# First stage of a hybrid attention block: scaling and copying x on ScalarE, small rows on ScalarE's DMA queue, gate weights loaded later and their products made up in steps 5 to 9

## What is computed

```
c_act = silu(c)
mod = c_act @ w_ada + b_ada
shift_m, scale_m, gate_m, shift_f, scale_f, gate_f = split(mod, 6)
h = rmsnorm(x, g_pre_mix) * (1.0 + scale_m) + shift_m
proj = h @ w_in
fq, fk, fv, ff, gq, gk, gv, ga, gr = split(proj, IN_OFFSETS)
log_f = log_sigmoid(ff + b_fgate)
cum = cumsum(log_f over the frames)      # bias of the attention logits: cum[q] - cum[k]
```

## Time and profile before

| | |
|---|---|
| three executions | 2312.43, 2312.89, 2318.76 us; median 2312.89 |
| profiled execution | 2309.94 us, of which the span (first to last instruction) is 2307.9 us |
| TensorE busy | 2173.3 us, 94% of the span |
| VectorE busy | 1520.3 us, 66% |
| ScalarE busy | 850.8 us, 37% |
| DMA | 441.09 MB, mean 191 GB/s |

### The profile page before, as it was taken

The page is one execution under the profiler, slowest core; times in us unless marked ns, Lnnn a source line. Parts: engine busy times, 40 slices in busy tenths (PEclk is TensorE's granted clock), DMA queues, the critical chain, the costliest instruction groups (busy, mean ns, idle before and its releaser), DMA issues.

```text
span 2307.9 us, 26312 instructions
## 1 busy us (share of the span) xinstructions
PE 2173.3 (94%) x9751; PEld 1769.3 (77%) x9751; DVE 1520.3 (66%) x1470; ACT 850.8 (37%) x1063; POOL 385.1 (17%) x217
## 2 busy tenths in 40 slices
PE   2778999999999999799999999999999999999996
PEld 2556877777777678688888888888878888888875
DVE  5855665666667732564454454454498989898998
ACT  2223323333333322443444343343344444444443
POOL 0000000000000000100000000000034545454664
PEclk9889999999999999899999999999999999999998
DMA  9855565555545342556666566566247664666763
GB/s 314 296 186 168 170 191 178 162 175 178 164 128 173 110 164 95 165 173 196 199 223 207 193 222 215 183 220 226 92 152 247 216 208 161 239 219 218 256 221 144
DMA packets 261821, 441.09 MB, mean 191 GB/s; under 512 B 17676, under 2 KB 110032, under 8 KB 255704
## 3 DMA queue, kind: packets, MB, share of 16 engines
q1 hardware_dynamic: 261128, 435.51, 56.6%
q10 hardware_dynamic: 592, 4.21, 0.5%
HBM read 379.88 MB, written 59.79 MB: 191 GB/s over the span
## 4 chain that ended last, share of the span: by engine, by line
PE 78%; issue 8%; DVE 7%; DVEq 2%; DMA 1%; SPq 1%; POOL 1%; ACT 1%; POOLq 0%; ACTq 0%
PE pair L737 25%; PE pair L739 24%; PE pair L738 24%; DVE am_acc L1721 3%; DVE v_op L1940 1%; DMA af_item<-in_w_ada 1%; PE pair L832 1%; DVEq L1720 1%; PE pair L811 1%; DVE w_lo L1485 0%; DVEq L1591 0%; PE pair L926 0%; POOL v_raw L2162 0%; PE pair L1008 0%; PE pair L872 0%
## 5 line engine op out<-in xcount | busy, mean ns | idle before, releaser
L737 PE MATMUL pair<-in_hi,w_hi 128*128 128x512 f32 x1792 | 725.3, 405 | 4.5 <-DVE grp L1496 2.5
L739 PE MATMUL pair<-in_hi,w_lo 128*128 128x512 f32 x1792 | 702.8, 392 | 0.0
L738 PE MATMUL pair<-in_lo,w_hi 128*128 128x512 f32 x1792 | 702.4, 392 | 0.0
L1485 DVE TENSOR_TENSOR w_lo<-w_raw,w_hi 128x2048 fp32r<-128x2048 f32 (+1 forms) x142 | 292.1, 2057 | 397.4 <-ACT w_hi L1101 396.8
L1101 ACT ACTIVATE w_hi<-w_raw 128x2048 fp32r<-128x2048 f32 (+1 forms) x142 | 244.7, 1723 | 461.6 <-PE pair L739 424.8
L737 PEld LDWEIGHTS pair<-in_hi,w_hi 128*128 128x128 f32 x1792 | 339.6, 190 | 86.3 <-issue 12.0
L739 PEld LDWEIGHTS pair<-in_hi,w_lo 128*128 128x128 f32 x1792 | 338.6, 189 | 73.3
L738 PEld LDWEIGHTS pair<-in_lo,w_hi 128*128 128x128 f32 x1792 | 339.6, 190 | 70.2 <-issue 2.6
L737 PE MATMUL pair<-v_op,hid_r 128*128 128x512 f32 x896 | 349.8, 390 | 5.8 <-DVE hid_r L1916 4.5
L738 PE MATMUL pair<-v_op,hid_r 128*128 128x512 f32 x896 | 349.2, 390 | 0.0
L739 PE MATMUL pair<-v_op,hid_r 128*128 128x512 f32 x896 | 349.1, 390 | 0.0
(11 more groups left out here) (205 smaller groups left out, 1880.3 us busy)
## 6 DMA issues: line engine op xcount, KB each, us to landing
w_raw<-in_w_mlp_in SPq DMA_DIRECT2D x64, 1024.0 KB, 5.3
v_raw<-in_w_mlp_out SPq DMA_DIRECT2D x128, 512.0 KB, 5.1
hid_r<-hid_scratch SPq DMA_DIRECT2D x112, 512.0 KB, 6.3
hid_scratch<-hid_r SPq DMA_DIRECT2D x28, 1792.0 KB, 7.2
am_item<-in_w_ada SPq DMA_DIRECT2D x64, 512.0 KB, 5.1
w_raw<-in_w_in SPq DMA_DIRECT2D x128, 256.0 KB, 3.4
af_item<-in_w_ada SPq DMA_DIRECT2D x64, 512.0 KB, 5.8
w_raw<-in_w_in SPq DMA_DIRECT2D x128, 128.0 KB, 3.2
```

Of the source, the lines that this page charges most:

```text
L737: pe.matmul(dst, a[0], b[0], start=start, stop=False, skip_group_check=onto)
L738: pe.matmul(dst, a[0], b[1], start=False, stop=False, skip_group_check=onto)
L739: return pe.matmul(dst, a[1], b[0], start=False, stop=stop, skip_group_check=onto)
L1485: dve.tensor_tensor(w_lo[n][:, view], w_raw[n][:, view], w_hi[n][:, view].bitcast(F32), ALU.subtract)\
```

## The change

1. The nine small row DMAs leave SP's queue and are issued by ScalarE as its first instructions. Their transposes use bank 5, and the x transposes wait for `cols_ready`.
2. ScalarE scales the four x tiles and copies all 16 transposed tiles out; VectorE does neither. VectorE has the block's eight items one after the other.
3. SP's order becomes: c, items and x as before up to item 7, then group 0's first weights (`load_fox(0, 0)`, 0.79 MB), item 8, the second weights, items 9 to 11, the two gate weight DMAs, and the rest.
4. The gate products of steps 0 to 4 are left out there and made up in steps 5 to 9, two in each. `wm_hi` moves to ahead of `modulate(4)`, `wm_lo` to the second block.
5. Item 16, block 2's first, is added ahead of `mod_columns_m(1)`, and item 24, block 3's first, ahead of `mod_columns_m(2)`. In blocks 1 to 3 the low part of the next weights stands right behind `mod_columns_m`, ahead of the first `in_lo`.
6. At the seam, `w_hi` and `w_lo` of group 1's first weights are made ahead of the `log_f` work, VectorE copies two tiles while it waits for the logarithm, and TensorE begins group 1's step 0 without `cum_ready`: it transposes `f_z` after three of the six tiles. Group 1 is written out instead of being the first pass of a loop.

```
@@ SP
-            load_am(2)
-            load_am(3)
-            for n, src in enumerate((g_pre_mix[0:1, :], b_ada[0:1, SHIFT_M:SHIFT_M + D],
...
-            load_am(4)
-            sp.wait_ge(wm_zero, 1)
-            sp.dma_start(wm_raw[:, :, 0:RANK], w_in_t[:, :, GA_COL:GA_COL + RANK]).then_inc(wm_in, 16)
...
+            for n in range(2, 8):
+                load_am(n)
             load_fox(0, 0, wait=False)
-            load_am(6)
-            load_am(7)
+            load_am(8)
             load_fox(0, 1, wait=False)
-            for n in range(8, 32):
+            for n in range(9, 32):
                 load_am(n)
+                if n == 11:
+                    sp.wait_ge(wm_zero, 1)
+                    sp.dma_start(wm_raw[:, :, 0:RANK], w_in_t[:, :, GA_COL:GA_COL + RANK]).then_inc(wm_in, 16)
@@ PE
             for k in range(KT):
                 if k == 0:
                     pe.wait_ge(xn_ready, TB)
+                    pe.wait_ge(cols_ready, 1)
                 if k >= TILES:
-                    pe.wait_ge((xt_act, xt_dve)[k % 2], (k - TILES) // 2 + 1)
+                    pe.wait_ge(xt_act, k - TILES + 1)
...
+            MISC_AT = [()] * 5 + [(2 * n, 2 * n + 1) for n in range(5)] + [(k,) for k in range(10, KT)]
...
+            def first_fox_slot(s):
+                if s == 0:
+                    pe.wait_ge(cum_ready, 1)
...
+                    last.then_inc(cumq_tr, 1)
+                    fox_value(0)
+                else:
+                    fox_slots(0)(s)
+
+            def first_logit():
+                pe.wait_ge(cumq_ready, 1)
+                fox_logit(0, 0)
+
+            group_steps(1, False, first_fox_slot, early=first_logit)
+            with pe.Fori(2, FOX_GROUPS) as r:
@@ ACT
+            for n, src in enumerate((g_pre_mix[0:1, :], b_ada[0:1, SHIFT_M:SHIFT_M + D],
...
+                as_rows(rows_a[n * KT:(n + 1) * KT, :], src)
...
+            def scale_x(t):
+                act.wait_ge(x_rstd, t + 1)
+                act.activation(x_raw[:, t, :], x_raw[:, t, :], ACT.Copy, scale=rstd[:, t:t + 1]).then_inc(xn_ready, 1)
...
+                if t:
+                    scale_x(t - 1)
+            scale_x(TB - 1)
+            for k in range(KT):
                 act.wait_ge(x_tr, k + 1)
                 act.activation(xn_t[:, k, :], bank[k % TILES][:, :], ACT.Copy).then_inc(xt_act, 1)
...
+                if k == 4:
+                    act.wait_ge(wm_in, 32)
+                    act.activation(wm_hi[:, :, :], wm_raw[:, :, :], ACT.Copy).then_inc(wm_hid, 1)
                 modulate(k)
...
+            split_hi(MM_G, arrived_group(1, 0), 0, NARROW)
             act.wait_ge(fz_abs, 1)
...
-            split_hi(MM_G, arrived_group(1, 0), 0, NARROW)
             evict_group(0, True)
@@ DVE
-            for t in range(TB):
-                dve.wait_ge(x_rstd, t + 1)
-                dve.tensor_scalar(x_raw[:, t, :], x_raw[:, t, :], rstd[:, t:t + 1], None, ALU.mult)\
-                    .then_inc(xn_ready, 1)
...
-            for k in range(1, KT, 2):
-                dve.wait_ge(x_tr, k + 1)
-                dve.tensor_copy(xn_t[:, k, :], bank[k % TILES][:, :]).then_inc(xt_dve, 1)
...
+            for block in range(KT // 4):
+                mod_columns_m(block)
+                if block == 0:
+                    first_lo(0)
+                else:
+                    split_lo(2 * block, 0, NARROW)
...
+                if more:
+                    for i in range(4, 9 if block < KT // 4 - 2 else 8):
+                        add_am(n + i)
             dve.wait_ge(am_used, 32)
 
+            split_lo(MM_G, 0, NARROW)
             dve.wait_ge(misc_sum, 1)
...
+            evict_group(0, True, slice(1, 4, 2))
             dve.wait_ge(fz_ln, 1)
```

More of the change, by code:

```diff
@@ L739, in split_mm, with group_steps @@
                 return pe.matmul(dst, a[1], b[0], start=False, stop=stop, skip_group_check=onto)
-            def group_steps(r, first, slot, misc_step=None):
+            def group_steps(r, first, slot, misc_step=None, early=None):
                 for k in range(KT):
@@ L752, in group_steps @@
                         pe.wait_ge(mod_lo, k + 1)
-                        misc_step(k)
+                        for n in MISC_AT[k]:
+                            misc_step(n)
                     for b in range(TILES):
@@ L766, in group_steps @@
                             slot(2 * k)
+                        if early and k == 0 and b == 4:
+                            early()
                     if not first:
@@ L786, in ada_rows, with fox_value, fox_logit @@
                 pe.matmul(dst[:, 0:2 * P], ones[:, :], acc[:, :], start=True, stop=True).then_inc(ada_sum, 1)
+            def fox_value(f):
+                pe.wait_ge(ev_act, 3 * f + 3)
+                pe.wait_ge(ev_dve, 3 * f + 3)
+                for t in range(TB):
+                    last = pe.transpose(BB[:, t * P:t * P + P], grp[:, VA, t * P:t * P + P], ident[:, :])
+                last.then_inc(fox_v_tr, 1)
+            def fox_logit(f, j):
+                i = j % TB
+                if j:
+                    pe.wait_ge(fox_max, 8 * f + j)
+                if j == 1:
+                    pe.wait_ge(fox_v_tok, 2 * f + 2)
+                if j == 0:
+                    pe.wait_ge(am_col, f + F_COL)
+                q_tile, k_tile = (QA, KA) if j < TB else (QB, KB)
+                pe.matmul(BA[:, 0:(i + 1) * P], grp[:, q_tile, i * P:i * P + P], grp[:, k_tile, 0:(i + 1) * P],
+                          start=True, stop=True).then_inc(fox_qk, 1)
             def fox_slot(s, f):
                 if s == 0:
-                    pe.wait_ge(ev_act, 3 * f + 3)
-                    pe.wait_ge(ev_dve, 3 * f + 3)
-                    for t in range(TB):
-                        last = pe.transpose(BB[:, t * P:t * P + P], grp[:, VA, t * P:t * P + P], ident[:, :])
-                    last.then_inc(fox_v_tr, 1)
+                    fox_value(f)
                 if s == 1:
@@ L801, in fox_slot @@
                 if s % 3 == 0 and s // 3 < 8:
[L802 to L811, removed]
-                              start=True, stop=True).then_inc(fox_qk, 1)
+                    fox_logit(f, s // 3)
                 if s % 3 == 2 and s // 3 < 8:
@@ L949, in fox_slots @@
                 return slot
-            pe.wait_ge(cum_ready, 1)
-            for t in range(TB):
-                last = pe.transpose(BA[:, t * FOX_HEADS:(t + 1) * FOX_HEADS], f_z[32:40, t * P:t * P + P],
-                                    ident[32:40, 32:40])
-            last.then_inc(cumq_tr, 1)
-            pe.wait_ge(cumq_ready, 1)
-            with pe.Fori(1, FOX_GROUPS) as r:
+            def first_fox_slot(s):
+                if s == 0:
+                    pe.wait_ge(cum_ready, 1)
+                    for t in range(TB):
+                        last = pe.transpose(BA[:, t * FOX_HEADS:(t + 1) * FOX_HEADS],
+                                            f_z[32:40, t * P:t * P + P], ident[32:40, 32:40])
+                    last.then_inc(cumq_tr, 1)
[7 more added lines that the diff above has]
+            with pe.Fori(2, FOX_GROUPS) as r:
                 group_steps(r, False, fox_slots(r - 1))
@@ L1486, in split_lo, with evict_group @@
                     .then_inc(lo_done, 1)
-            def evict_group(r, scaled):
-                for b in range(1, TILES, 2):
+            def evict_group(r, scaled, tiles=slice(1, TILES, 2)):
+                for b in range(TILES)[tiles]:
                     if b < TILES - 1:
```

87 lines of the change are left out of this document (38 added, 49 removed).

## The result

| | before | changed |
|---|---|---|
| median of the executions | 2314.65 us (4: 2312.43 to 2318.76) | 2295.81 us (4: 2294.46 to 2295.94) |
| profiled execution, its span | 2309.94, 2307.9 us | 2295.91, 2294.1 us |

The ratio is 0.9915, with a 95% interval of 0.9898 to 0.9932: 18.8 us less by the medians. The median forecast was 2293.7, the range 2287 to 2301. The forecast counted from the 2312.89 us of three executions; a fourth moved that median to 2314.65, and against 2312.89 the gain is 17.1 us.

A forecast was written before the change was run, and what follows sets the result against it. It took VectorE's list, with the DMA stream close behind, to bound the kernel. 20.2 us at the fourth columns less 1.0 for the seam's clock gave 19.2: profiled 2309.94 to 2290.7, plus 2.95, median 2293.7; range 2287 to 2301.

The forecast's parts named there:

- First columns: Block 0: VectorE takes items 2 to 7 from 22.0 to 38.5, then 2.6 us; columns at 41.1 instead of 58.7.
- The x path: Opening, ScalarE: scalings to 26.6, copies to between 36 and 41, taken as 37, beside item 7's end at 38.5.
- Fourth columns: Block 3's columns, end of the first stage: 133.3 instead of 153.5, 20.2 us less.
- The stream's path is the later one: DMA up to item 31: 34.9 MB at 354 GB/s plus 3.7 us; lands 126.9, columns 132.6, plus 0.7.
- the one that took 7.2 off for waits "now filled": Later blocks, VectorE: waits for the sum and `in_hi` filled by moved work; 94.8 us becomes 87.6.
- VectorE's path: First to fourth columns by VectorE's own work: 41.1 + 87.6 = 128.7.
- The moved cost: Gate weights' short runs: 3.7 us of stream time moved from the opening into block 1, not removed.
- the range's other end: Rival, chance 0.2: stream stops at block starts, 1.5 us each, and for gate weights; gain 10 to 14, median 2299 to 2303.
- The count of made-up products: TensorE, block 0 and after: 18 matmuls fewer in steps 0 to 4, up to 6 more in each of 5 to 9; no cost.
- The seam: Group 0 to 1: gain up to 4.9 us not banked, chain stays 16.4, hole moves behind row maximum, clock costs 1.0.
- The likeliest case: Whole kernel: 20.2 - 1.0 = 19.2 us less, median 2293.7, own range 2290 to 2297, chance 0.55.
- the one with the stream not the limit: Rival, chance 0.2: stream at 379 GB/s, VectorE's 128.7 decides; 24.8 us off, median 2288, or 2286.

The follow-up runs named there:

- the experiment with x alone: Only the x scaling and the copies moved to ScalarE, against the kernel before: ratio 0.9965 (0.9948 to 0.9981), median 2304.84 us.
- the version with both edits: Changed kernel with group 0's cumulative sums broadcast by TensorE and gate weights behind item 16: 2285.16 us, ratio 0.9885; 2288.87 beside the changed kernel's 2297.14.

## Why 19 us and not more, and why the prediction held

**First columns: right.** 41.1 was worked out for their completion, and they begin at 40.63 and are complete at 41.09. Its terms held: item 2 from 22.2 (22.0 forecast), item 7 ended at 38.5 (38.5), from there to the columns 2.6 (2.6). The last term is partly luck: with the same order of work its wait was 2.10 to 3.54 us in other executions, and the first columns began between 40.5 and 42.2. The x path, with scalings of 1.99 and copies to 37.9, stayed 0.6 us inside its cover. Of the Trainium skill's rule on multiplications ("ScalarE: Activation LUTs", Rules for kernel authors) the experiment with x alone decides: ScalarE is slower per tile (1.99 against 1.22 us) and the kernel gained 9.6 us at the fourth columns, since VectorE was the engine waited for. That run moves the copies too; the multiplications alone were not run.

**Fourth columns: the number right, its path half right.** 133.3 was forecast for their completion, 133.25 measured (they begin at 132.79). "The stream's path is the later one" holds for the second block alone. There the gate weights' short runs cost what was said: 30 us x (1 - 331/381) = 3.9 against 3.7, and SP was held 9.87 us for them (7.31 before). VectorE waited 3.2 us for it. From 75 us on VectorE set the pace, for a reason that can be added up. Between first and fourth columns it took 94.49 us before and 92.16 after. Its waits fell only from 9.72 to 9.13: those for the sum from 6.64 to 4.06, those for `in_hi` from 3.08 to 1.86, and 3.21 for items are new. The other 1.75 is one `w_lo`, which now stands behind the fourth columns. The step that failed is the one that took 7.2 off for waits "now filled"; 3.8 was true. The sum's wait was taken as filled whole by one item put ahead of it (1.58 and 0.44 were left), and that for `in_hi` as filled whole by `w_lo` (0.61 was left each time, for the second `in_lo` of a block and no longer the first). The `w_lo` that went past the fourth columns, 1.75, was not counted, and made up half. VectorE's path alone is thus 40.63 + 94.49 - 3.80 - 1.75 = 129.6 to the start of the fourth columns, and the kernel without the gate weights' loads, where no item is waited for, has them at 130.06. With the 3.2 us of the second block it is 132.8. The forecast had this path complete at 128.7, 1.3 us too early (130.0 by the same sum), and let the stream's path end the stage at 132.6, with 0.7 added. That 133.3 came out is in part luck: VectorE's path and the waits of the second block happen to add up to the same. The stream's path was sized right but does not end the stage: item 31 is issued from 119.23 on, its second half about 119.6, and such items land 6.7 us later, at 126.3 (126.9 forecast), and VectorE has used it only at 130.75.

**The moved cost.** The gate weights late win nothing alone (1.0001), and without their loads the fourth columns would come 2.7 us earlier. The move was no gain in this stage, as the sum had it; the range's other end, 4.5 us of holes at the block starts, did not come: from 33 to 48, from 75 to 80 and from 105 to 110 the share is 1.05 to 1.07. The count of made-up products was off, without effect: 15 matmuls fewer in steps 0 to 4, not 18, and 3 more in each of steps 5 to 9, not 6.

**The seam: the mechanism right, its cost too small.** Right that nothing is banked: undoing it costs nothing. Right too that the hole moves behind the row maximum and takes the clock with it. But the sum has 1.0 us for the clock and nothing for the chain, and together they cost 2.9. The clock's part is 2.06 (8.65 us against 6.59 for the same matmuls), above even the 0 to 1.4 that was allowed. The chain: from the gate product to TensorE's resume 16.4 us was forecast and it took 17.25. Up to the store of the sums into DRAM it takes 6.87 us with the seam rewritten (160.41 - 153.54) and with the seam as before (159.25 - 152.38) alike; the way through DRAM up to ScalarE's next instruction then took 7.64 and 6.67. So the 0.9 us more lies in the transfer. It need not be the seam's doing: over the profiled kernels this way took 6.67 to 7.51 us with the old seam and 6.77 to 8.23 with the new one. What sets it is open.

**The sum.** 19.2 us was forecast and the medians gave 18.8. In the two profiled executions the lead is 20.3 at the fourth columns (20.2 forecast), 20.5 at the last gate product, 19.6 at TensorE's resume, 17.6 at the second row maximum, 13.8 at the end. So by the trace the changed code is worth 17.6 us where the sum had 19.2; what the pair loses from there to 13.8 arises behind it. The medians allow either, within their interval of 0.0034 (8 us); that they agree with the forecast to 0.4 us is luck. The likeliest case came about for the most part; of the rivals, the one with the stream not the limit was right on the mechanism from 75 us on, and wrong on the time.

**The signs.** Two things that were to show the prediction wrong did appear: a hole in the stream (172 GB/s from 48 to 54) and a rate at full share outside 340 to 370 (387 and 375 from 24 to 48). They make up for each other, with 351 in the mean where 354 was taken, so the time did not show them. The third, the chain changing by over 1 us, stayed just below with 0.9.

## What the runs showed of the chip that was not expected

Time behind the change is no constant. The stretch from the first row maximum to the end of the fourth group, the same work each time (1563 matmuls on record), in the kernel before, the changed one, and the changed one again:

```profile
190.19:527.32 337.13, 322.74 (x1563) 261.62 (x1563) 208.39 (x434) 106.94 (x181) 17.63 (x32) 0.99 0.56 175
```

```profile
170.58:510.41 339.83, 326.28 (x1563) 264.29 (x1563) 208.45 (x435) 106.99 (x181) 17.56 (x32) 0.98 0.54 174
```

```profile
170.97:515.02 344.05, 330.91 (x1563) 267.99 (x1563) 208.60 (x435) 107.03 (x181) 17.57 (x32) 0.97 0.54 172
```

The 2.7 us between the first two are mostly the clock behind the row maximum, 2.06 us; from the second row maximum on the two differ by 0.6 (330.54 and 331.18). The second and third are one kernel: 4.2 us apart in this stretch, and 4.2 at the end of the program (2294.1 and 2298.3), with the fourth columns 0.14 apart. The granted clock goes with it. In steps of 5 us the changed kernel's second execution has these below 0.8 behind the second row maximum:

```profile
200.00:205.00 5.00, 5.00 (x19) 3.98 (x18) 3.48 (x6) 0.79 (x2) 0.55 (x1) 0.68 0.54 126
285.00:290.00 5.00, 4.13 (x16) 3.63 (x17) 2.72 (x10) 1.11 (x3) 0.55 (x1) 0.66 0.55 157
375.00:380.00 5.00, 5.00 (x20) 3.99 (x20) 3.13 (x6) 1.53 (x2) 0.55 (x1) 0.77 0.53 158
460.00:465.00 5.00, 5.00 (x23) 4.22 (x22) 3.48 (x6) 0.78 (x3) 0.55 (x1) 0.74 0.47 118
```

The first execution has the first two of them and not the others; the kernel before has one in the same stretch, at 215. Both executions have the fall to 0.50 at 170 to 175, behind their waits of 6.08 and 6.13 us. Whether such a hole is followed by the 1.2 GHz level is not a matter of its length alone. The same place, in the kernel before and in the changed one:

```profile
303.00 0.30 PE L841 MATMUL pair<-ident,f_o 128*128 128x128 f32 x1 [2.89 <-DVE f_o L1613]
303.14 0.83 PE L832 MATMUL pair<-fv_tok,prob_t 128*128 128x128 f32 x6
303.73 0.48 PE L737 MATMUL pair<-in_hi,w_hi 128*128 128x512 f32 x1
304.04 0.40 PE L738 MATMUL pair<-in_lo,w_hi 128*128 128x512 f32 x1
```

```profile
284.19 0.30 PE L839 MATMUL pair<-ident,f_o 128*128 128x128 f32 x1 [2.32 <-DVE f_o L1636]
284.32 1.33 PE L830 MATMUL pair<-fv_tok,prob_t 128*128 128x128 f32 x6
285.31 0.77 PE L725 MATMUL pair<-in_hi,w_hi 128*128 128x512 f32 x1
285.88 0.63 PE L726 MATMUL pair<-in_lo,w_hi 128*128 128x512 f32 x1
```

The hole of 2.89 us was followed by matmuls of 0.40, the shorter one of 2.32 by matmuls of 0.63 for some three microseconds. Over all kernels profiled the stretch from the second row maximum to the end of the fourth group took 328 to 338 us. That is as large as the effects of most single edits here. Of the 5.8 us of lead that the profiled pair lost behind TensorE's resume, 2.1 are thus the changed kernel's own, 0.6 lie in this stretch, and 3.4 went between 738 and 961 us (223.02 us against 219.59), where the granted clock's mean reads 0.95 in both (0.3 came back behind it). Why is open, but two executions of the version with both edits differ as much in that part of the program: 206.7 us from 729.03 to 935.75, and 209.8 from 731.78 to 941.60. What decides whether the clock falls at a hole of 2 to 3 us was not found; behind the waits of 5.2 to 6.7 us at the seam it fell in all six executions.

## What to carry to other kernels

Where several limits lie close, work out each path by itself, but list the waits that a reordering leaves over as well as those it fills: an item or a `w_lo` put ahead of a wait shortens it by what the other engine doesn't need longer, not by its whole length. Moving work to an engine that is slower at it pays when the engine it leaves is the one waited for. A gain at a seam counts only at the next place where the same chain is waited for, and one long wait there can cost more than the shorter ones it replaces: 2 us here, by the clock of the matmuls behind it. Judge single edits by landmarks in the trace, the last of them behind such a wait, and the whole by many executions, since one profiled pair can be about 5 us off the medians.
